# Two fused transformer blocks on one core: gate evacuation, key sums, roots and last stores moved in a written schedule

## The chip, the cores and the metric

The kernel runs as one program on one core of a Trainium2 chip. The metric is the device time of one execution in microseconds (us), taken from the chip and not from a host. Three executions of the kernel before are given, and one further execution that the hardware profiler recorded. The core has five engines that matter here: TensorE (PE, matrix products into eight PSUM banks), VectorE (DVE), ScalarE (ACT), GpSimd (POOL) and SyncE (SP, which only issues transfers). Each runs its own list of instructions in order, and they meet by semaphores.

## The reference, cut to what matters

The computation is two transformer-like blocks over 512 tokens of width 1024, in fp32, one behind the other. What the change touches lies in the hybrid mixer at the front of the first block, in the first norm of the second block, and in the last norm.

```python
def hybrid_mixer(h, w_in, ...):
    proj = h @ w_in
    gu, gv, q, k, v, gate, b_logit, a_logit = split_cols(proj, IN_SIZES)
    y_a = chunk_spatial_gating(gu, gv, gm_ln_g, gm_ln_b, gm_ws, gm_bs)
    qkv = silu(causal_dwconv(concatenate([q, k, v]), dn_conv))     # 4 taps
    q, k = l2norm(q), l2norm(k)                                    # per head
    g = -exp(dn_a_log) * softplus(a_logit + dn_dt_bias)
    o = gated_delta_rule(q, k, v, g, sigmoid(b_logit))             # 4 heads, 4 chunks of 128 tokens
    o = rmsnorm(o, dn_onorm) * silu(gate)
    return concatenate([y_a, o]) @ w_out
# gated_delta_rule, per head, chunk: decay = cumsum(g); m = strict(k_beta k^T * exp(decay_i - decay_j));
# solve (I + m) sol = [v_beta, k_beta exp(decay)]; then a recurrence over the chunks
def first_block(x, mem, ...):
    x = x + hybrid_mixer(rmsnorm(x), ...)
    x = x + memory_cross_attention(rmsnorm(x), rmsnorm(mem), ...)
    x = x + squared_relu_mlp(rmsnorm(x), ...)
    return rmsnorm(x, norm_final)
def second_block(x, ...):
    u = rmsnorm_2(x); proj = u @ w_in_2 + b_in_2    # conv branch, window attention (q, k, v with rope), merged
    x = x + merged @ w_mix_out;  x = x + (silu(conv(up)) * gate) @ w_ffn_down
    return rmsnorm_2(x)
```

## The kernel before, in words

**Products.** Every projection of 1024 (or fewer) input channels onto 128 output channels is a list of k-tiles (`KT` is 8), and each k-tile is three matrix products that together make an fp32 result: weight high part by activation high part, high by low, low by high (lines 1308 to 1310). One such product over 512 tokens takes about 0.23 us of PE, so half a projection, 12 products, takes 2.7 to 2.9 us. The high part of each weight tile is made by ACT (line 1604) and the low part by DVE (line 1884), four slots ahead; together these two are a "split".

**One list sets the order.** The function `schedule` writes one list of steps, and each engine's program walks that same list and emits its own part of each step. So a step that stands earlier in the list stands earlier on every engine that it uses. The steps around the change, with the lines of their instructions:

- `mm` is a piece of a projection. Its result lies in one of four projection banks, taken in turn, number j modulo 4. A bank is free again only when the step that evacuates it has run.
- `conv` evacuates a projection of q, k or v (DVE L1869), then ACT applies the first tap (L1667) and DVE the other three (L1876); `shape` is its silu on ACT (L1671).
- `gate` evacuates an output gate of the mixer (DVE L1869, into `gate`) and applies silu to it (ACT L1707).
- `sums` transposes a head's queries or keys on PE (L1381) and squares and sums them on ACT (L1679); DVE finishes them (L1974), and `norms` makes the scales (DVE L1980 to L1986).
- `decays` makes the cumulated decays of all heads (PE L1369, L1370; DVE L1954, L1957). `decay` of a head spreads them (PE L1235), and exponentiates (ACT L1713, with a table load; DVE L2030, L2034; ACT L1716).
- `strict` makes the strictly triangular matrix of a head (PE L1411, L1412; DVE L2042 to L2059), `turn` transposes the first inverse (PE L1420, DVE L2062), and `level_y` and `level_x` (PE L1437 and L1465, L1470; ACT L1721; DVE L2069, L2089, L2090) double the size of the inverted blocks, in six levels. At level 6 `level_y` has eight transposes with it (L1448, L1449), that DVE turns into `strict_t`, `decays_t` and `k_dec` (L2079 to L2082). `solve` closes a head. Two heads are on their way at a time, under the numbers 0 and 1 of their tiles.
- `statistics`, `normalise` and `mix` are the spatial gating of one group: transposes (PE L1388), mean and variance (DVE L2000 to L2004), normalising (DVE L2010), product. `mix_bias` is PE L1374 and DVE L1961.
- `square`, `root` and `row` are a norm: sums of squares tile by tile, then transposes and the root, then the row of scales spread over the partitions. In the first norm of the second block, `square` adds on POOL (L2344), with a second sum on POOL beside it (L2352), `root` is PE L1229 with small work on DVE and POOL (L2335, L2357), and `row` is PE L1235.

**Side banks.** The results of the small PE steps (`sums`, `decay`, `strict`, `turn`, levels, `statistics`, `mix`) share the other four PSUM banks, 4 to 7. They are given out in rotation, in the order of the list: a step takes the bank after the one before it, and PE waits until whoever read that bank last is done. So a step moved in the list changes which banks the steps behind it take, and for whom they wait.

**What sets the pace of the small steps.** `delta_head` is a generator that yields after each small step of a head; the main loop draws one piece of projection work (half a projection) from `filler`, then one step of each head in flight. The list `aside` holds small steps that are taken one at a time, one behind each half projection (`halves_and_aside`). So a step more in `aside` puts all behind it half a projection later.

**The end.** The last norm is applied to the second half of the tokens in parts, one DVE multiplication and one store for each part: `LAST_TILES` lists the k-tiles of a part (DVE L2319; the stores are issued by the queues of ACT, L1848, and SP, L2420).

## Time and profile before

| quantity | value |
|---|---|
| three executions | 1566.84, 1570.03, 1570.04 us; median 1570.03 us |
| the profiled execution | 1569.95 us |
| its span | 1568.2 us (1.75 us lie around it) |
| granted clock of TensorE, mean over the span | 0.993 |
| busy PE, DVE, ACT, POOL | 98%, 56%, 38%, 7% of the span |
| bytes moved | 146.70 MB, 94 GB/s on the mean |

The busy shares are means over the span. PE is busy nearly all of it, so the time can shrink only where PE stands still, where its clock is down, or at the two ends. A list of waits shows for whom an engine stood still and how long; the timeline shows each instruction with its start, its length, and, in brackets, the idle time right before it with the instruction that ended it. A row with "x4" groups four instructions. The granted clock is 1.00 at TensorE's full 2.4 GHz and 0.50 at 1.2 GHz.

### The profile page before, as it was taken

How to read it: one execution, taken by the hardware profiler on the slowest of the kernel's cores; microseconds unless marked ns; L12 is line 12 of the kernel's file. 1: busy time of each engine (PE TensorE's matmuls, PEld its weight loads, DVE VectorE, ACT ScalarE, POOL GpSimd, SP SyncE). 2: the span in 40 equal slices, each digit the busy share in tenths (PEclk: the TensorE clock that was granted, in tenths of full speed). 3: DMA queues.
4: the chain of work that ended last, by engine and by line, in shares of the span. 5: the costliest groups of instructions: out<-in, count | busy, mean ns of one | idle time of the engine just before them, and what ended most of it. 6: DMA issues, size and time to landing. Idle time of an engine off the chain costs nothing.

```text
span 1568.2 us, 20461 instructions
## 1 busy us (share of the span) xinstructions
PE 1543.0 (98%) x8150; PEld 1275.4 (81%) x8150; DVE 878.0 (56%) x1331; ACT 601.8 (38%) x975; POOL 104.9 (7%) x91
## 2 busy tenths in 40 slices
PE   9898999999999999999999999999999999999998
PEld 7687789888788888888888877877888888888887
DVE  7676666654364344445565777644555663564465
ACT  6534333533344132322446344432334331332233
POOL 0000111220030000000040010100002000000000
PEclk9998999999999999999999999999999999999999
DMA  7211113531132322232332223221332233222221
GB/s 265 68 55 41 55 55 109 188 107 59 36 113 90 107 90 99 94 104 78 108 108 81 81 81 108 74 94 62 107 113 89 95 107 102 87 99 102 95 71 64
DMA packets 44941, 146.70 MB, mean 94 GB/s; under 512 B 5040, under 2 KB 8368, under 8 KB 44720
## 3 DMA queue, kind: packets, MB, share of 16 engines
q1 hardware_dynamic: 42448, 141.80, 26.8%
q10 hardware_dynamic: 2400, 3.61, 0.7%
q8 instruction: 65, 1.06, 0.3%
q14 instruction: 28, 0.23, 0.1%
HBM read 143.29 MB, written 2.10 MB: 93 GB/s over the span
## 4 chain that ended last, share of the span: by engine, by line
PE 87%; DVE 6%; ACT 4%; issue 3%; DMA 1%; POOL 0%; SPq 0%; DVEq 0%; POOLq 0%; ACTq 0%
PE bank L1308 26%; PE bank L1310 26%; PE bank L1309 26%; DVE w_lo L1884 1%; PE bank L1526 1%; PE bank L1543 1%; ACT w_hi L1604 1%; DVE temp L1876 1%; PE bank L1437 1%; PE bank L1465 1%; DVE temp L1869 1%; PE bank L1470 1%; PE bank L1273 0%; PE bank L1275 0%; PE bank L1274 0%
## 5 line engine op out<-in xcount | busy, mean ns | idle before, releaser
L1308 PE MATMUL bank<-a_hi,w_hi 128*128 128x512 f32 (+1 forms) x1275 | 499.3, 392 | 6.0 <-DVE gate L1869 6.0
L1310 PE MATMUL bank<-a_hi,w_lo 128*128 128x512 f32 (+1 forms) x1275 | 491.3, 385 | 0.0
L1309 PE MATMUL bank<-a_lo,w_hi 128*128 128x512 f32 (+1 forms) x1275 | 491.2, 385 | 0.0
L1884 DVE TENSOR_TENSOR w_lo<-w_raw,w_hi 128x1024 fp32r<-128x1024 f32 (+2 forms) x259 | 330.3, 1276 | 171.4 <-ACT w_hi L1604 171.0
L1604 ACT ACTIVATE w_hi<-w_raw 128x1024 fp32r<-128x1024 f32 (+2 forms) x259 | 267.0, 1034 | 198.3 <-PE bank L1310 195.0
L1308 PEld LDWEIGHTS bank<-a_hi,w_hi 128*128 128x128 f32 x1275 | 240.6, 189 | 57.5 <-issue 9.9
L1310 PEld LDWEIGHTS bank<-a_hi,w_lo 128*128 128x128 f32 x1275 | 240.4, 189 | 48.5
L1309 PEld LDWEIGHTS bank<-a_lo,w_hi 128*128 128x128 f32 x1275 | 240.9, 189 | 45.6
L1308 PE MATMUL bank<-b_hi,w_hi 128*128 128x512 f32 (+1 forms) x720 | 276.7, 384 | 0.4 <-ACT b_hi L1744 0.4
L1309 PE MATMUL bank<-b_lo,w_hi 128*128 128x512 f32 (+1 forms) x720 | 275.1, 382 | 0.0
L1310 PE MATMUL bank<-b_hi,w_lo 128*128 128x512 f32 (+1 forms) x720 | 275.1, 382 | 0.0
L1308 PEld LDWEIGHTS bank<-b_hi,w_hi 128*128 128x128 f32 x720 | 135.3, 188 | 28.4 <-issue 1.7
L1310 PEld LDWEIGHTS bank<-b_hi,w_lo 128*128 128x128 f32 x720 | 135.3, 188 | 26.3
L1309 PEld LDWEIGHTS bank<-b_lo,w_hi 128*128 128x128 f32 x720 | 135.4, 188 | 26.1 <-issue 0.2
L2156 DVE TENSOR_TENSOR xs<-xs,bank 128x512 f32<-128x512 f32 (+1 forms) x88 | 55.9, 637 | 135.0 <-PE bank L1310 130.9
L1869 DVE TENSOR_TENSOR temp<-bank,rstd 128x512 f32<-128x512 f32 x101 | 69.4, 687 | 62.5 <-PE bank L1310 58.0
L1876 DVE SCALAR_TENSOR_TENSOR temp<-temp,columns 128x512 f32<-128x512 f32 x96 | 72.3, 753 | 35.0 <-ACT temp L1841 17.2
L2344 POOL TENSOR_TENSOR square_sum<-square_sum,square 128x512 f32<-128x512 f32 x28 | 39.5, 1410 | 612.5 <-ACT square L1639 612.5
L2134 DVE TENSOR_TENSOR b_lo<-temp,b_hi 128x512 fp32r<-128x512 f32 x62 | 42.9, 692 | 59.3 <-ACT b_hi L1744 59.0
L1744 ACT ACTIVATE b_hi<-temp 128x512 fp32r<-128x512 f32 x62 | 39.2, 633 | 82.5 <-DVE temp L2313 56.7
L1784 ACT ACTIVATE temp<-temp 128x512 f32<-128x512 f32 x32 | 20.2, 632 | 89.4 <-DVE temp L2209 89.4
L2335 POOL TENSOR_TENSOR narrow<-narrow,columns 128x4 f32<-128x4 f32 (+1 forms) x13 | 18.5, 1423 | 422.0 <-DVE narrow L1927 382.9
(317 smaller groups left out, 1196.2 us busy)
## 6 DMA issues: line engine op xcount, KB each, us to landing
w_raw<-weights_in SPq DMA_DIRECT2D x247, 512.0 KB, 3.2
w_raw<-weights_in SPq DMA_DIRECT2D x8, 384.0 KB, 2.9
x_first<-x_in SPq DMA_DIRECT2D x8, 256.0 KB, 5.8
xs<-x_in ACTq DMA_DIRECT2D x8, 256.0 KB, 5.0
w_raw<-weights_in SPq DMA_DIRECT2D x8, 256.0 KB, 2.7
mem_x<-mem_in SPq DMA_DIRECT2D x1, 1024.0 KB, 7.7
out<-xs SPq DMA_DIRECT2D x8, 128.0 KB, 1.8
w_raw<-front_in SPq DMA_DIRECT2D x5, 192.0 KB, 6.1
```

Of the source, the lines that this page charges most:

```text
L1308: pe.matmul(to, weights_hi[:, at], hi, start=k == k0, stop=False)
L1309: pe.matmul(to, weights_hi[:, at], lo, start=False, stop=False)
L1310: t = pe.matmul(to, weights_lo[:, at], hi, start=False, stop=k == k1 - 1)
L1604: act.activation(split_weights(n)[0][:, 0:size], raw[:, n % SLOTS, 0:size], ACT.Copy).then_inc(split_act.handle, 1)
L1744: act.activation(b_hi[:, b_slot(g, i), :], x, ACT.Copy).then_inc(b_act.handle, 1)
L1784: act.activation(temp("relu", n), temp("relu", n), ACT.Square).then_inc(relu_act.handle, 1)
L1869: return dve.tensor_tensor(to, full(name, n, k0)[0:to.shape[0], 0:width], scale[0:to.shape[0], 0:width], ALU.mult)
L1876: dve.scalar_tensor_tensor(acc, buf[:, at:at + S], weight(i), acc, ALU.mult, ALU.add).then_inc(done.handle, 1)
L1884: dve.tensor_tensor(lo[:, 0:size], raw[:, n % SLOTS, 0:size], hi[:, 0:size].bitcast(F32), ALU.subtract).then_inc(split_dve.handle, 1)
L2134: dve.tensor_tensor(lo, x, hi.bitcast(F32), ALU.subtract).then_inc(b_dve.handle, 1)
L2156: dve.tensor_tensor(xs[:, t, tokens], xs[:, t, tokens], full(name, t, k0)[:, 0:tokens.stop - tokens.start], ALU.add).then_inc(residual_dve ...
L2344: pool.tensor_tensor(total, total, square("square", n)[:, 0:total.shape[1]], ALU.add).then_inc(square_pool.handle, 1)
```

## The change

It has five parts. The first is at the front. The gates 0 and 1 are no longer taken from `aside` behind later half projections; their evacuation (`gate`) stands right behind `decays`, and their silu is a step of its own (`silu`) behind the silu of the third convolution of head 0. The projection that runs ahead is cut 2, 3, 3 k-tiles instead of 1, 5, 2. The queries' `sums 0` stands behind `strict 0` (it is `next(first)` a second time that puts it there), so that head 0, and with it every head behind it, is one step further ahead of the projections. Splits are taken at most one at a time.

The second is in the later heads: for heads 2 and 3 an empty entry is put into `aside` between the queries' and the keys' `sums`, so that the keys' stand half a projection later; the norms follow one entry on. The third is an empty entry ahead of the first `mix`. The fourth is at the first norm of the second block: the two `root` steps stand half a k2 projection and half a q2 projection earlier. The fifth cuts the last norm's parts from three (3, 3, 2 tiles) into four (1, 2, 3, 2 tiles).

```diff
@@ -59,7 +59,7 @@
 
 ON_DVE = (A_INPUT, *HALF_OF)
 
-LAST_TILES = [slice(0, 3), slice(3, 6), slice(6, KT)]
+LAST_TILES = [slice(0, 1), slice(1, 3), slice(3, 6), slice(6, KT)]
 
 
 
@@ -196,19 +196,20 @@
     def add(kind, n=0):
         out.append((kind, n))
 
-    def split_ahead(j):
-        while split[0] < min(j + LEAD + 1, N_LOADS) and (split[0] < SLOTS or split[0] - SLOTS in done or (
-                split[0] >= FIRST_EXTRA and PROJ["gate2", F2T - 1, 0] in done)):
-            add("split", split[0])
-            split[0] += 1
-
-    def project(name, n, k0=0, ka=None, kb=None):
+    def split_ahead(j, most=SLOTS):
+        for _ in range(most):
+            if split[0] < min(j + LEAD + 1, N_LOADS) and (split[0] < SLOTS or split[0] - SLOTS in done or (
+                    split[0] >= FIRST_EXTRA and PROJ["gate2", F2T - 1, 0] in done)):
+                add("split", split[0])
+                split[0] += 1
+
+    def project(name, n, k0=0, ka=None, kb=None, most=SLOTS):
         j = PROJ[name, n, k0]
         ka, kb = WEIGHTS[j][2] if ka is None else ka, WEIGHTS[j][3] if kb is None else kb
         if j < FRONT:
             done.add(j)
             return
-        split_ahead(j)
+        split_ahead(j, most)
         add("mm", (j, ka, kb))
         if kb == WEIGHTS[j][3]:
             done.add(j)
@@ -220,13 +221,13 @@
     aside, convolved, normed_heads = [], [], []
 
     def halves_and_aside(name, n):
-        project(name, n, kb=KT // 2)
+        project(name, n, kb=KT // 2, most=1)
         while convolved:
             add("shape", convolved.pop(0))
         if aside:
             aside.pop(0)()
         yield
-        project(name, n, ka=KT // 2)
+        project(name, n, ka=KT // 2, most=1)
         if aside:
             aside.pop(0)()
 
@@ -245,11 +246,15 @@
         for h in range(1, H):
             yield from conv_qkv(h)
             yield from conv_qkv(H + h)
-            aside.extend([lambda h=h: add("sums", h), lambda h=h: add("sums", H + h), lambda h=h: scaled(h)])
+            aside.append(lambda h=h: add("sums", h))
+            if h > 1:
+                aside.append(lambda: None)
+            aside.extend([lambda h=h: add("sums", H + h), lambda h=h: scaled(h)])
             yield from conv_qkv(2 * H + h)
             for n in GATES_BEHIND.get(h, ()):
                 yield from halves_and_aside("gate", n)
                 add("gate", n)
+                add("silu", n)
                 yield
         norm = memory_norm()
         for n in range(H):
@@ -261,7 +266,10 @@
                     add("spatial_u", n)
                 else:
                     add("spatial_v", n)
-                    aside.extend([lambda n=n: add("statistics", n), lambda n=n: add("normalise", n), lambda n=n: add("mix", n)])
+                    aside.extend([lambda n=n: add("statistics", n), lambda n=n: add("normalise", n)])
+                    if n == 0:
+                        aside.append(lambda: None)
+                    aside.append(lambda n=n: add("mix", n))
                 yield
                 if n or name == "gv":
                     next(norm, None)
@@ -273,6 +281,7 @@
         for _ in last:
             pass
         add("gate", H - 1)
+        add("silu", H - 1)
         yield
         while aside:
             aside.pop(0)()
@@ -374,19 +383,23 @@
     project("gate", 1, ka=KT // 2)
 
     ahead = PROJ["qkv", 1, 0]
-    add("mm", (ahead, 0, 1))
+    add("mm", (ahead, 0, 2))
     add("sums", H)
     add("decays")
-    add("mm", (ahead, 1, KT - 2))
+    for n in GATES_BEHIND[0]:
+        add("gate", n)
+    add("mm", (ahead, 2, 5))
     first = delta_head(0)
     next(first)
-    add("mm", (ahead, KT - 2, KT))
+    add("mm", (ahead, 5, KT))
     done.add(ahead)
+    scaled(0)
+    next(first)
     add("sums", 0)
-    scaled(0)
     add("shape", 2 * H)
+    for n in GATES_BEHIND[0]:
+        add("silu", n)
     filler = itertools.chain(projections(), first_memory_keys())
-    aside.extend([lambda: add("gate", 0), lambda: add("gate", 1)])
     in_flight, waiting = [first], list(range(1, H))
     while waiting or in_flight:
         next(filler, None)
@@ -471,11 +484,11 @@
             if k1 == FT:
                 normed(A_SECOND, n)
                 add("square2", n)
-    project("k2", 0)
+    project("k2", 0, kb=KT // 2)
     add("root", A_SECOND)
-    project("q2", 0, kb=KT // 2)
+    project("k2", 0, ka=KT // 2)
     add("root", A_TWICE)
-    project("q2", 0, ka=KT // 2)
+    project("q2", 0)
     add("row", A_SECOND)
 
     for n in (QT, 0):
@@ -1002,7 +1015,7 @@
-        gate_dve, gate_act = signal("gate_dve", "gate"), signal("gate_act", "gate")
+        gate_dve, gate_act = signal("gate_dve", "gate"), signal("gate_act", "silu")
@@ -1702,7 +1715,7 @@
-                elif kind == "gate":
+                elif kind == "silu":
                     q.wait_ge(*gate_dve.at(n))
                     act.activation(gate[:, n, :], gate[:, n, :], ACT.Silu).then_inc(gate_act.handle, 1)
```

The lines of the new kernel are 13 higher than those of the old from `project` on: L1869 is L1882, L1420 is L1433, and so on. Three places in the order of the instructions follow. In all of them `temp3`, `bank7` and the like are names with the number of the buffer.

**VectorE, from the decays of head 0 to its first turn.** Before, from the copy of the decays (L1954) on:

```order
L1954 COPY small<-bank5 128x32
L1957 TENSOR_TENSOR small<-small 128x16
L2030 TENSOR_TENSOR decays_t0<-bank6,small 128x512
L2034 TENSOR_TENSOR decays_t0<-decays_t0,matrices 128x512
...
L2047 TENSOR_TENSOR strict_b0<-bank4,decays_t0 64x256 x2
...
L1869 TENSOR_TENSOR temp3<-bank1,rstd 128x512
...
L1876 SCALAR_TENSOR_TENSOR temp4<-temp3,columns,temp4 128x512 x3
L1884 TENSOR_TENSOR w_lo<-w_raw,w_hi 128x1024 x2
L1869 TENSOR_TENSOR gate<-bank3,rstd 128x512
L1869 TENSOR_TENSOR gate<-bank0,rstd 128x512
L2062 COPY inv_b0<-bank6 128x256
```

Now, from the same copy on:

```order
L1967 COPY small<-bank5 128x32
L1970 TENSOR_TENSOR small<-small 128x16
L1882 TENSOR_TENSOR gate<-bank3,rstd 128x512
L1882 TENSOR_TENSOR gate<-bank0,rstd 128x512
L2043 TENSOR_TENSOR decays_t0<-bank6,small 128x512
...
L2060 TENSOR_TENSOR strict_b0<-bank7,decays_t0 64x256 x2
...
L1987 TENSOR_SCALAR narrow<-narrow 128x4
L1882 TENSOR_TENSOR temp3<-bank1,rstd 128x512
...
L1889 SCALAR_TENSOR_TENSOR temp4<-temp3,columns,temp4 128x512 x3
L1897 TENSOR_TENSOR w_lo<-w_raw,w_hi 128x1024
L2075 COPY inv_b0<-bank6 128x256
L1897 TENSOR_TENSOR w_lo<-w_raw,w_hi 128x1024
```

The two evacuations into `gate` have moved from behind two splits of weights, and behind the convolution, to a place ahead of the first multiplication of `decays_t0`. The copy into `inv_b0`, which is the turn of head 0, now has one split (`w_lo`) ahead of it rather than two and the gates.

**ScalarE, in the middle of heads 1 and 2.** `square0` or `square1` with `narrow` is the sum of squares of the keys or queries, `decays_t0` is head 2, `level_y1` is head 1. Before:

```order
L1671 ACTIVATE qkv<-temp4 128x512
L1679 ACTIVATE square1,narrow<-bank4 128x128 x4
L1721 ACTIVATE level_y1<-bank5 128x256
L1713 ACT_TABLE_LOAD
...
L1716 ACTIVATE decays_t0<-decays_t0 128x512
L1679 ACTIVATE square0,narrow<-bank7 128x128 x4
L1667 ACTIVATE temp2<-temp1,columns 128x512
L1604 ACTIVATE w_hi<-w_raw 128x1024
L1671 ACT_TABLE_LOAD
L1671 ACTIVATE qkv<-temp2 128x512
L1721 ACTIVATE level_y1<-bank4 64x256
```

Now:

```order
L1734 ACTIVATE level_y1<-bank5 128x256
L1726 ACT_TABLE_LOAD
...
L1729 ACTIVATE decays_t0<-decays_t0 128x512
L1680 ACTIVATE temp0<-temp4,columns 128x512
...
L1684 ACTIVATE qkv<-temp0 128x512
L1692 ACTIVATE square1,narrow<-bank5 128x128 x4
L1734 ACTIVATE level_y1<-bank6 128x256
L1680 ACTIVATE temp2<-temp1,columns 128x512
L1617 ACTIVATE w_hi<-w_raw 128x1024
L1684 ACTIVATE qkv<-temp2 128x512
L1692 ACTIVATE square0,narrow<-bank7 128x128 x4
L1734 ACTIVATE level_y1<-bank4 64x256
```

The exponential of head 2's decay (the first table load) stands one silu, one group of squares and one `level_y1` earlier, and the keys' squares from bank 7, once ahead of a scale, a split and a silu, stand behind all of them. On TensorE the first turn of head 2, which read bank 5 before, now takes bank 7. Before, on TensorE:

```order
L1448 MATMUL bank5<-matrices,qkv 128x128
L1449 MATMUL bank6<-matrices,qkv 128x128
L1308 MATMUL bank3<-a_hi,w_hi 128x512
...
L1374 MATMUL bank7<-ws,matrices 128x512 [waits strict_dve,ws_pool]
L1459 MATMUL bank4<-inv_t1,level_y1 64x64 [waits level_y_act]
L1459 MATMUL bank4<-inv_t1,level_y1 64x64 x3
L1420 MATMUL bank5<-matrices,inv_tb0 64x64 [waits level_y_dve]
L1420 MATMUL bank5<-matrices,inv_tb0 64x64 x7
L1308 MATMUL bank0<-a_hi,w_hi 128x512 [waits conv_dve,split_dve,split_act]
```

Now:

```order
L1462 MATMUL bank6<-matrices,qkv 128x128
L1461 MATMUL bank5<-matrices,qkv 128x128
L1462 MATMUL bank6<-matrices,qkv 128x128
L1433 MATMUL bank7<-matrices,inv_tb0 64x64 [waits sums_act]
L1433 MATMUL bank7<-matrices,inv_tb0 64x64 x7
L1321 MATMUL bank3<-a_hi,w_hi 128x512
...
L1387 MATMUL bank4<-ws,matrices 128x512 [waits level_y_act,ws_pool]
L1472 MATMUL bank5<-inv_t1,level_y1 64x64 [waits level_y_dve]
L1472 MATMUL bank5<-inv_t1,level_y1 64x64 x3
L1450 MATMUL bank6<-inv_b0,level_b01 64x64 [waits turn_dve]
```

The turn of head 2 stood behind the product of `ws` (`mix_bias`) and waited for DVE's `level_y_dve`; now it stands right behind the transposes and waits for `sums_act`, ACT's squares of that bank 7.

**TensorE, at the projections k2 and q2 and the roots.** Before, the last products of k2, the first root, half of q2, the second root:

```order
L1308 MATMUL bank0<-a_hi,w_hi 128x512 [waits stage_dve,stage_act]
...
L1308 MATMUL bank0<-a_hi,w_hi 128x512 [waits stage_dve,stage_act]
...
L1229 MATMUL bank4<-matrices,square_sum 128x128 [waits square_pool]
L1229 MATMUL bank4<-matrices,square_sum 128x128 x3
L1308 MATMUL bank1<-a_hi,w_hi 128x512 [waits residual_dve,split_dve,split_act]
...
L1229 MATMUL bank5<-matrices,square_sum2 128x128 [waits square2_pool]
L1229 MATMUL bank5<-matrices,square_sum2 128x128 x3
L1308 MATMUL bank1<-a_hi,w_hi 128x512
...
L1235 MATMUL bank6<-matrices,narrow 128x128 [waits root_dve,root_pool]
```
Now:

```order
L1321 MATMUL bank0<-a_hi,w_hi 128x512 [waits stage_dve,stage_act]
L1242 MATMUL bank7<-matrices,square_sum 128x128 [waits square_pool]
L1242 MATMUL bank7<-matrices,square_sum 128x128 x3
L1321 MATMUL bank0<-a_hi,w_hi 128x512 [waits stage_dve,stage_act]
...
L1321 MATMUL bank0<-a_hi,w_hi 128x512 [waits stage_dve,stage_act]
L1242 MATMUL bank4<-matrices,square_sum2 128x128 [waits square2_pool]
L1242 MATMUL bank4<-matrices,square_sum2 128x128 x3
L1321 MATMUL bank1<-a_hi,w_hi 128x512 [waits residual_dve,split_dve,split_act]
...
L1321 MATMUL bank1<-a_hi,w_hi 128x512
L1248 MATMUL bank5<-matrices,narrow 128x128 [waits root_dve,root_pool]
```
`bank7<-matrices,square_sum` (four transposes of the first root) stood behind all 24 products of k2 and now stands behind 12 of them, half a projection earlier; the second root likewise. The row (`narrow`, last of what is shown) stands behind the whole of q2 as before.

## Rows read from the trace of the kernel before

**Rows 1.** Waits of TensorE: engine, line, waited for, us in all, times, longest.

```profile
PE bank L1308 <- DVE gate L1869: 6.0, 1, 6.0
...
PE bank L1420 <- DVE k_dec L2082: 1.7, 1, 1.7
...
PE bank L1459 <- ACT level_y L1721: 0.5, 1, 0.5
```

**Rows 2.** Windows: busy us (instructions) PE, PEld, DVE, ACT, POOL; clock; DMA share; GB/s.

```profile
55.74:62.57 6.83, 2.89 (x7) 2.34 (x8) 5.96 (x10) 3.73 (x6) 0.00 (x0) 0.50 0.46 152
137.66:141.07 3.41, 3.41 (x17) 3.41 (x17) 1.64 (x5) 0.00 (x0) 0.93 (x1) 0.50 0.00 0
151.31:158.14 6.83, 6.21 (x28) 5.03 (x29) 4.41 (x10) 1.57 (x2) 0.00 (x0) 0.50 0.23 82
171.79:175.20 3.41, 2.04 (x37) 1.50 (x36) 3.19 (x8) 2.30 (x3) 0.00 (x0) 1.00 0.00 0
```

**Rows 3.** Timeline, TensorE, head 0: start, length, line, tiles, [idle before <- its ender].

```profile
39.02 0.63 PE L1381 MATMUL bank<-matrices,qkv 128*128 128x128 f32 x4 [0.63 <-ACT qkv L1671]
...
59.68 0.76 PE L1308 MATMUL bank<-a_hi,w_hi 128*128 128x512 f32 x1 [6.05 <-DVE gate L1869]
...
64.97 0.50 PE L1308 MATMUL bank<-a_hi,w_hi 128*128 128x512 f32 x1
...
67.86 0.60 PE L1381 MATMUL bank<-matrices,qkv 128*128 128x128 f32 x4
...
69.46 0.50 PE L1308 MATMUL bank<-a_hi,w_hi 128*128 128x512 f32 x1
```

**Rows 4.** Timeline, VectorE, strict 0 and the convolution behind it.

```profile
49.29 0.88 DVE L2047 TENSOR_TENSOR strict_b<-bank,decays_t 64x256 f32<-64x256 f32 x2
...
52.86 0.68 DVE L1869 TENSOR_TENSOR temp<-bank,rstd 128x512 f32<-128x512 f32 x1
...
56.58 2.35 DVE L1884 TENSOR_TENSOR w_lo<-w_raw,w_hi 128x1024 fp32r<-128x1024 f32 x2
```

**Rows 5.** Timeline, TensorE, heads 1 and 2.

```profile
124.61 0.68 PE L1465 MATMUL bank<-inv_tb,level_y 64*64 64x64 f32 x16
...
137.44 0.56 PE L1411 MATMUL bank<-qkv 128*128 128x128 f32 x2 [2.84 <-ACT square L1679]
...
145.20 0.48 PE L1308 MATMUL bank<-a_hi,w_hi 128*128 128x512 f32 x1
```

**Rows 6.** Timeline, ScalarE, head 2's decay and the squares of its keys.

```profile
132.27 1.28 ACT L1713 ACT_TABLE_LOAD   x1
133.56 0.60 ACT L1713 ACTIVATE temp<-bank 128x512 f32<-128x512 f32 x1
...
136.18 0.26 ACT L1679 ACTIVATE square<-bank 128x128 f32<-128x128 f32 x1
```

**Rows 7.** Timeline, TensorE, from the transposes of statistics 0.

```profile
167.63 0.60 PE L1388 MATMUL bank<-matrices,temp 128*128 128x128 f32 x4
...
174.18 0.68 PE L1470 MATMUL bank<-level_y,inv_tb 64*64 64x64 f32 x16 [1.37 <-DVE temp L2010]
```

**Rows 8.** Timeline, VectorE, normalise 0.

```profile
172.76 1.36 DVE L2010 TENSOR_SCALAR temp<-bank,ln_mean 128x128 f32<-128x128 f32 x4
```

**Rows 9.** Timeline, TensorE, k2, the roots and the row.

```profile
809.65 0.39 PE L1308 MATMUL bank<-a_hi,w_hi 128*128 128x512 f32 x1
...
815.09 0.60 PE L1229 MATMUL bank<-matrices,square_sum 128*128 128x128 f32 x4
...
822.60 1.09 PE L1235 MATMUL bank<-matrices,narrow 128*128 128x128 f32 x8 [0.96 <-POOL narrow L2357]
```

**Rows 10.** Timeline, GpSimd, its last square sum before the root.

```profile
813.45 1.40 POOL L2344 TENSOR_TENSOR square_sum<-square_sum,square 128x512 f32<-128x512 f32 x1 [3.04 <-ACT square L1639]
```

**Rows 11.** Timeline, VectorE, the last multiplications.

```profile
1562.33 2.42 DVE L2319 TENSOR_TENSOR xs<-xs,bank 128x768 f32<-128x768 f32 x3 [1.30 <-PE bank L1235]
```

**Rows 12.** Windows, the end: columns as in the second group.

```profile
1564.25:1567.45 3.20, 0.00 (x0) 0.00 (x0) 0.49 (x1) 0.00 (x0) 0.00 (x0) 0.53 0.97 328
```


## The prediction

> **What bounds the kernel now.** I read the busy shares first: TensorE is busy 98% of the span, so of the profiled 1569.95 us only its idle time, its slow clock and the two ends are to be had. Then the waits of TensorE in the part that the change moves: 6.0 us at a projection for DVE's evacuation of a gate, 1.7 us for `k_dec`, 0.5 us for ACT's `level_y` [rows 1]. Then the timeline around each, with the instruction that ended it. At 59.68 TensorE resumes after 6.05 us [rows 3]: this projection needs bank 3, which gate 0 (L1869) still holds. At 137.44 it resumes after 2.84 us for squares on ACT [rows 5], at 174.18 after 1.37 us for `normalise 0` [rows 7], at 822.60 after 0.96 us for a root on GpSimd [rows 9]. Last the granted clock, by windows: it is 0.50, that is 1.2 GHz, in 55.74 to 62.57, 137.66 to 141.07 and 151.31 to 158.14, each at or right behind a stall, and 1.00 in 171.79 to 175.20, which holds the 1.37 us stall [rows 2]. At half clock TensorE's busy time there is twice what it need be: losses of 2.89/2 = 1.4, 3.41/2 = 1.7 and 6.21/2 = 3.1 us. So a stall costs its length, and, if it is like the larger ones, 1.4 to 3.1 us behind it.
>
> Unit prices. Half a projection between small steps is 64.97 to 67.86 = 2.9 us; one group of four transposes with one `level_x` is 67.86 to 69.46 = 1.6 us [rows 3], which I divide 0.5 and 1.1 by their instructions. On DVE the strict matrix takes 49.29 to 52.86 = 3.6 us, a convolution, from its evacuation until its taps are done, 52.86 to 56.58 = 3.7 us [rows 4]. Four squares with their sums take 136.18 to 137.44 = 1.3 us on ACT [rows 5, 6].
>
> **Part 1, front, head 0.** Removed: the 6.05 us stall and 1.4 us of slow clock, and the 0.63 us that `sums 4` waits [rows 1 to 3]; 8.1 us in all. Added on DVE are two evacuations (the same instruction at 52.86 takes 0.68 us, and the next can start some 0.6 after it) before the first `decays_t` multiplication, where DVE waits for ACT's exponential anyway; they need the bank of gate 1, whose products have ended by then. I cost them at nothing; if that cover were gone they would be 1.2 to 1.4 us on the way to `strict 0`. What is late next is the turn of head 0: it is issued one piece of projection earlier on TensorE, but its copy on DVE stands behind conv 1 and one split. DVE starts on the strict matrix when TensorE has made it, which is 2.6 us earlier than 49.29, since the queries' four transposes and squares are no longer ahead. Then come 3.6 us of strict, 3.7 us of convolution and one split (half of the 2.35 us of the pair at 56.58, so 1.2 [rows 4]), and the copy, 0.4: 46.7 + 3.6 + 3.7 + 1.2 + 0.4 is 55.6, and with 0.25 us for the start of conv 1's taps behind ACT, which now also has the silus of both gates to do, 55.9. TensorE has by then done its projections and stands at `level_y (0, 1)` from 53.3. Stall 2.6 us, about as long as the 2.84 us one, so I add the slow clock of that size, 1.4 to 1.7: 4.1, with 0.3 for small waits at `decay 0` 4.4. Gain 8.1 - 4.4 = 3.7. Bounds: 6.5 if the clock holds and the stall is 1.2 shorter; 1 if both silus and the second split come ahead of the copy (1.2 + 1.2 us and more slow clock).
>
> **Part 2, later key sums, with head 2 one step ahead.** Removed: 2.84 + 1.7 at 137.44, then 0.5 + 1.7 + 3.1 around 151.93 [rows 1, 2, 5]: 9.8 us. Added: `decay 2` now stands ahead of conv 7 on DVE and of its silu on ACT, and the first turn of head 2 takes the bank of the keys' squares `sums 7`, which stand on ACT behind the silu of conv 11. From the start of the exponential's table load: DVE has its two multiplications done after about 3.3 (the exponentials end 0.6 before 136.18, 132.27 to 136.18 being 3.9 [rows 6]); conv 7 3.7; silu 0.6 and squares 1.3; one multiplication 0.7; strict 3.6; updates of the last level 1.2; conv 11 3.7; silu 0.6; squares 1.3. Sum 20.0 us. TensorE from the same moment: between `level_x (1, 4)` at 124.61 and the stall's start at 134.60 lie 10.0 us [rows 5]; less that `level_x` and one spread (1.1 + 0.4) 8.5, plus `strict 2`, half a projection and the last `level_y` with its transposes, which fill 137.44 to 145.20 less the slow clock's 1.7 = 6.1: 14.6, plus two short waits behind DVE and ACT, 0.9 together, 15.5 to 15.9. Stall 4.2 us, slow clock 1.7 as behind the 2.84 us stall, small waits 0.9: 6.9 us with rounding. The old stall at the `mix_bias` end goes, for the head is a step ahead. Gain 9.8 - 6.9 = 2.9. Bounds: 9.8 if ACT gets to the squares in time; -1 if the clock loss is the 3.1 us one and DVE lags one split (1.2) and an evacuation more.
>
> At this place the Trainium skill has a rule that speaks against the change, since more chains now wait behind an exponential. The row: the table load takes 1.28 us and the ACTIVATE starts right behind it, 132.27 + 1.28 = 133.55 against 133.56 [rows 6]. The page "ScalarE: Activation LUTs", section "What ACT_TABLE_LOAD costs", puts a switch at 1.283 us of load and 1.380 us of drain, 2.66 us. By that rule this stall would be 1.4 us longer and the sum of all parts 1.4 us worse; the trace has no such drain at the row, so the sum keeps 1.28.
>
> **Part 3, first mix later, heads 2 and 3.** `level_y (2, 3)` now takes the bank of `statistics 0`, free when `normalise 0` is done. Before, that was 167.63 to 172.76 + 1.36 = 174.12, 6.5 us after the statistics began [rows 7, 8]; the two updates of `level_x (2, 2)` now stand ahead, so I take 7.0. TensorE needs 0.5 (statistics) + 1.1 + 0.4 + 2.9 = 4.9. Stall 2.1 against 1.4 before; I price the slow clock at 0.7, half of the least seen, since none came behind 1.37 us and one came behind 2.84. Two more short waits behind `k_turn` and `normalise` of the next head, where each bank moves on by one, I take at 0.9 together. New loss 1.4 + 1.1 over before with the clock: 2.4. Bounds: 0 to -5 (another stall of 2.8 with its clock).
>
> **Part 4, roots half a projection earlier.** GpSimd's last square sum ends at 813.45 + 1.40 = 814.85 [rows 10]. The first half of k2 is done at 809.65 + (815.09 - 809.65)/2 = 812.4 [rows 9]. Before, the root came at 815.09 and found its sum ready by 0.2 us; now TensorE waits 2.5 us. Then remain half of k2, q2 whole and two roots: 3 halves of 2.8 with 0.7 for the roots, row at 824.1. Before it came at 822.60, behind a wait of 0.96, so the root's chain is no longer what it waits for. Loss 824.1 - 822.6 = 1.5, and 1.3 of slow clock for a stall just under 2.84: -2.8. Bounds: -1.5 (no clock), -4.6 (3.1).
>
> **Part 5, last stores.** The three multiplications take 2.42 us from 1562.33 [rows 11], and the stores' data run from 1564.25 to 1567.45 at a share of 0.97 [rows 12]: the transfer is the bound, and its start follows the first part. With one tile first instead of three, 2/8 of 2.42 = 0.6 us less before the first issue. A fourth issue costs some 0.1 to 0.6, and unless one queue serves two short stores better than one, I keep +0.2, from -0.3 to +0.6. The same skill's page "DMA: Bandwidth & Descriptors", section "Anatomy of one DMA", gives about 2.0 us fixed for each DMA (on GpSimd's path). By it a further store that lay alone would cost 2.0; the packets at 0.97 show that fixed times overlap here. I keep +0.2.
>
> **Sum.** 3.7 + 2.9 - 2.4 - 2.8 + 0.2 = +1.6 us. 1569.95 - 1.6 = 1568.35; the median before is 0.08 above the profiled execution: 1568.4. A measurement of this kernel can tell about 0.2%, 3.1 us, from no change; the forecast lies within.
>
> **Rivals.**
> (a) The new waits are covered. The turn of head 2 finds its bank free, since ACT runs its scale and split earlier than I chain them, and `level_y (2, 3)` too. Then parts 2 and 3 are +9.8 - 1 (small waits) and 0, and the sum 3.7 + 8.8 - 2.8 + 0.2 = 9.9: 1560.1; with only half of that stall gone (2.1, and its 1.7 of clock) 1564.6. For it: DVE is busy 56% and ACT 38%, and each price above was put end to end. Against: the squares stand behind the silu, which stands behind the taps, in the order itself.
> (b) Slower. Stalls that start the slow clock: at the first root TensorE stands still 2.5 us in the midst of dense products, and if each of the new stalls (front 2.6, turn 4.2, level 2.1, root 2.5) draws the 3.1 us loss seen behind 151.93 in place of the 1.4, 1.7, 0.7 and 1.3 that I gave them, the loss grows by 7.3: 1575.7. From two of the four on, by about 3.3, it is 1571.7, slower than before. For it: the loss came behind a stall of 1.66 with 0.54 before it. Against: it was 1.4 and 1.7 behind longer ones.
> (c) It does nothing: the 6 us at the front only move to the turn's copy, because the splits behind it (`most=1`) hold DVE or the copy waits for conv 1 in full. Then part 1 is 0 to +1, the sum -1 to -2: 1571.5.
>
> **How the numbers follow.** Forecast 0.40: faster in 0.08 of it, within 0.2% in 0.27, slower in 0.05. (a) 0.32, nearly all faster. (b) 0.14, slower in 0.12. (c) 0.14: within 0.10, slower 0.04. Together faster 0.40, same 0.39, slower 0.21. The range reaches over (a)'s half case towards its end and over (b) from two stalls: 1561.0 to 1572.5; the forecast's own is 1565 to 1571.
>
> **What would show it.** In the new trace: no wait of a projection for a gate, and one of 2 to 3 us at the first `level_y` for the turn's copy; the wait for `sums` at the turn of head 2, about 4 us (its absence is (a)); a wait of some 2 us at `level_y (2, 3)` for `normalise`; 2.5 us at the first root for GpSimd's square sum, and none at the row; windows at 0.50 behind each. It would be wrong if the new waits are under 1 us each or if a stall over 3 us appears at a place that I don't name, in the later gating groups above all, where every bank has moved on.

## The result, and the profile after

The changed kernel takes 1572.4 us (median of 12 executions, 1569.5 to 1573.1), the kernel before 1569.1 us (12 executions, 1566.8 to 1570.6). The ratio is 1.0018, with a 95% interval of 1.0009 to 1.0026: the change makes the kernel slower by some 2.8 us (3.3 us by the medians). I had forecast 1568.4 us, 1.6 us faster than the profiled execution before, with a range of 1561.0 to 1572.5 us: the direction came out wrong, and the time at the range's slow end.

The profiled execution of the changed kernel took 1569.49 us, with a span of 1567.8 us; that of before took 1569.95 us. Read side by side, the two profiles say "0.5 us faster". How that goes with a slower median is the first lesson of this case. The waits of TensorE after the change (engine and line, waited for, us in all, times, the longest; lines are 13 higher than before):

```profile
PE bank L1433 <- ACT square L1692: 4.5, 1, 4.5
PE bank L1450 <- DVE temp L2023: 3.6, 2, 2.1
PE bank L1450 <- DVE inv_b L2075: 2.5, 1, 2.5
PE bank L1242 <- POOL square_sum L2357: 2.3, 1, 2.3
...
PE bank L1242 <- DVE k_dec L2095: 1.0, 1, 1.0
PE bank L1493 <- DVE temp L2023: 0.8, 1, 0.8
```

The 6.0 us wait for a gate, the 1.7 us one for `k_dec` and the 0.5 us one for `level_y` at its old place [rows 1] are gone, and so is the 2.8 us one for squares [rows 5]. In their place stand 4.5 us at the turn of head 2, 3.6 us in two waits for `normalise`, 2.5 us for the turn's copy of head 0 and 2.3 us for GpSimd's square sum. The timeline of TensorE at these places, with the wait in brackets:

```profile
55.49 0.68 PE L1450 MATMUL bank<-inv_b,level_b 64*64 64x64 f32 x16 [2.49 <-DVE inv_b L2075]
```

```profile
141.25 1.12 PE L1433 MATMUL bank<-matrices,inv_tb 64*64 64x64 f32 x16 [4.50 <-ACT square L1692]
```

```profile
168.20 0.68 PE L1450 MATMUL bank<-inv_b,level_b 64*64 64x64 f32 x16 [2.08 <-DVE temp L2023]
...
189.03 0.68 PE L1450 MATMUL bank<-inv_b,level_b 64*64 64x64 f32 x16 [1.50 <-DVE temp L2023]
...
202.71 0.41 PE L1242 MATMUL bank<-matrices,temp 128*128 128x128 f32 x2 [0.99 <-DVE k_dec L2095]
...
210.99 0.46 PE L1493 MATMUL bank<-inv_t,strict_t 128*128 128x128 f32 x2 [0.81 <-DVE temp L2023]
```

```profile
811.59 0.88 PE L1242 MATMUL bank<-matrices,square_sum 128*128 128x128 f32 x4 [2.35 <-POOL square_sum L2357]
```

The granted clock of the same execution, by windows (columns as in [rows 2]: busy us of PE, PEld, DVE, ACT, POOL, then the clock):

```profile
55.00:61.00 6.00, 5.51 (x66) 4.65 (x67) 4.91 (x10) 2.65 (x5) 0.00 (x0) 1.00 0.53 178
139.45:146.25 6.80, 5.00 (x25) 4.07 (x26) 3.91 (x11) 3.33 (x11) 1.01 (x1) 0.50 0.22 77
168.00:175.00 7.00, 6.80 (x78) 5.88 (x79) 5.59 (x13) 3.20 (x6) 1.27 (x2) 1.00 0.01 2
811.87:815.28 3.41, 3.41 (x12) 2.73 (x11) 2.76 (x3) 0.00 (x0) 1.44 (x2) 0.50 0.17 24
```

Half clock came at two of these four places (a last stretch, from 1562.8 us to the span's end, meets no work of TensorE; every profile has one at its end), for a loss of 5.00/2 + 3.41/2 = 4.2 us, against 6.2 us in the profiled execution before. Behind the 2.5 us wait at the front and the 2.1 us wait of the gating the clock stayed at 1.00. So the time without slow clock is 1569.95 - 6.2 = 1563.7 us before and 1569.49 - 4.2 = 1565.3 us after: on that scale the change costs 1.6 us. Beside the drawn clock, one execution can tell a difference to about 1 us, as the start of the kernel varies too (see the second profile below).

### The profile page after: what moved, and what is told of

The parts are those of the page before. It is cut to its first block, busy times and chain, and to the rows that moved or that the text cites. A ratio compares the mean times of both kernels' runs of the same rounds, so it can differ in the third digit from the quotient of the medians.

```text
span 1567.8 us, 20470 instructions
## 1 busy us (share of the span) xinstructions
PE 1542.2 (98%) x8150; PEld 1274.0 (81%) x8150; DVE 877.5 (56%) x1332; ACT 601.6 (38%) x975; POOL 104.8 (7%) x91
## 4 chain that ended last, share of the span: by engine, by line
PE 89%; issue 4%; DVE 4%; ACT 2%; POOL 1%; POOLq 0%; DVEq 0%; ACTq 0%
PE bank L1321 26%; PE bank L1322 26%; PE bank L1323 26%; PE bank L1539 1%; PE bank L1556 1%; DVE temp L1889 1%; POOL square_sum L2357 1%; PE bank L1478 1%; PE bank L1450 1%; PE bank L1286 0%; PE bank L1288 0%; PE bank L1287 0%; PE bank L1483 0%; DVE temp L1882 0%; PE bank L1596 0%
## 5 line engine op out<-in xcount | busy, mean ns | idle before, releaser
L2169 DVE TENSOR_TENSOR xs<-xs,bank 128x512 f32<-128x512 f32 (+1 forms) x88 | 55.9, 636 | 134.9 <-PE bank L1323 130.8
L1882 DVE TENSOR_TENSOR temp<-bank,rstd 128x512 f32<-128x512 f32 x101 | 69.3, 686 | 56.4 <-PE bank L1323 51.8
```

Of the source, the lines that this page charges most:

```text
L1882: return dve.tensor_tensor(to, full(name, n, k0)[0:to.shape[0], 0:width], scale[0:to.shape[0], 0:width], ALU.mult)
L2169: dve.tensor_tensor(xs[:, t, tokens], xs[:, t, tokens], full(name, t, k0)[:, 0:tokens.stop - tokens.start], ALU.add).then_inc(residual_dve ...
```

## The experiments

Twelve runs follow, of eleven edited kernels and of the changed one once more, with 5 to 11 executions each. They ran in three groups (the first on one chip, the other two on another), each with the kernel before beside it: the changed kernel, the roots, the key sums and the extra step; then the first mix, the front alone and two of the better versions; then the rest. The runs of before had medians of 1569.0, 1569.25 and 1569.0 us, so I compare across the groups, though the changed kernel ran only in the first. "Ratio" is to before, "below the changed kernel" is a difference of medians to its run here.

**The clock: the changed kernel again.** No edit.

> The changed kernel, unchanged, for a second profile and as the reference of its neighbours. The profile of the first was of an execution of 1569.5 us, and 8 of 12 executions took 1571.6 to 1573.1. Theory A (most executions have one more stretch at half clock, behind the 2.5 us wait at the front or the 2 us wait of the gating): median 1572.4, and a profiled execution above 1572 shows a third stretch at 0.50, worth about 2.9 us. Rival B (the difference is spread over the program, as transfers or slow starts): such a profile shows two stretches as the first did, and lags the first profile little by little.

Measured: 1571.8 us, ratio 1.0020 (1.0010 to 1.0030). Its profiled execution took 1571.6 us, 2.1 us more than the first, and has the same waits to within 0.1 us: 4.5, 3.6 in two, 2.5 and 2.4 us. Its windows:

```profile
56.13:59.54 3.41, 3.18 (x21) 2.71 (x22) 2.40 (x6) 1.50 (x4) 0.00 (x0) 0.50 0.69 205
141.45:148.27 6.82, 4.73 (x25) 3.85 (x26) 4.20 (x11) 3.32 (x11) 1.01 (x1) 0.50 0.21 77
813.87:817.28 3.41, 3.41 (x11) 2.82 (x12) 2.93 (x3) 0.00 (x0) 1.44 (x2) 0.50 0.07 18
```

A third stretch stands at the front. It is worth 3.18/2 = 1.6 us, not the 2.9 us that I expected; together 5.7 us, so 1565.9 us without slow clock, 0.6 us above the first profile. That rest lies at the start: the first transposes of head 0 begin at 39.40 us here and at 38.84 us in the first profile. Over the 13 profiles of the changed kernel and its variants, whose order is the same up to there, they begin between 38.8 and 40.0 us. This is Theory A, though the profiled execution was not one above 1572: the stalls are the same in each execution, and which of them draws half clock is not.

**The roots.** In the diffs of the experiments, + is what the experiment has and - what the changed kernel has.

```diff
-    project("k2", 0, kb=KT // 2)
+    project("k2", 0)
     add("root", A_SECOND)
-    project("k2", 0, ka=KT // 2)
+    project("q2", 0, kb=KT // 2)
     add("root", A_TWICE)
-    project("q2", 0)
+    project("q2", 0, ka=KT // 2)
```

> The changed kernel with only the k2/q2 roots put back where they stood. Theory A (the root now waits for GpSimd's square sum and pulls the slow clock behind it): the 2.3 us wait and the window at clock 0.50 behind it vanish, the row is at the old distance from k2's first product, and the time is 3.0 us below the changed kernel (1572.4), so about 1569.4, ratio to before 1.000. Rival B (that loss is given back later, since the row waited for GpSimd anyway): within 0.7 us of the changed kernel, 1572.

Measured: 1569.0 us, ratio 1.0004 (0.9995 to 1.0012), 2.7 us below the changed kernel beside it. The 2.3 us wait is gone, and the row waits 1.0 us for GpSimd again. Theory A holds: 3.0 expected, 2.7 found. Half of it is wait. The rest I put down to the clock: of the seven profiles that have the root's wait, four have a stretch of 3.4 us behind it, worth 1.7 us each, so 1.0 us on the mean. This one profile can't show it by itself, since it has three stretches of 3.4 us at other places: at the front, at the turn of head 2 and behind `statistics 0`.

**The key sums.**

```diff
             aside.append(lambda h=h: add("sums", h))
-            if h > 1:
-                aside.append(lambda: None)
             aside.extend([lambda h=h: add("sums", H + h), lambda h=h: scaled(h)])
```

> The changed kernel without the empty entry between a head's query and key sums. Theory A (turn 2 waits 4.5 us because the keys' squares of head 3 stand behind the silu of conv 11): the squares come half a projection earlier, ahead of that silu, the wait and the slow clock behind it (2.6 us) are gone, less 1 to 2 us for a next wait: 5 to 6 us below the changed kernel, about 1567. Rival B (DVE is late there whatever the squares do, as it has strict 2 and conv 11 in a row, and the wait only changes its name): the stall of 3 to 4.5 us stands at the first product of ws or at the turn with another releaser, and the time is within 1.5 us of the changed kernel.

Measured: 1568.6 us, ratio 0.9996 (0.9987 to 1.0005), 3.2 us below the changed kernel. The 4.5 us wait is gone, but two take its place, of 0.96 us at `level_x (1, 5)` for `strict 2` on DVE and of 1.12 us for `k_dec`:

```profile
134.79 0.68 PE L1481 MATMUL bank<-level_y,inv_tb 64*64 64x64 f32 x16 [0.96 <-DVE strict_t L2058]
...
145.60 0.50 PE L1470 MATMUL bank<-inv_t,level_y 64*64 64x64 f32 x5 [1.12 <-DVE k_dec L2093]
```

Between the two theories: the squares were the cause of the long wait, and DVE stands some 1 us behind them.

**The same squares, otherwise.** The step for the keys of head 3 and the silu of conv 11 swap places.

```diff
-        while convolved:
-            add("shape", convolved.pop(0))
-        if aside:
-            aside.pop(0)()
+        if convolved == [2 * H + 3]:
+            aside.pop(0)()
+            add("shape", convolved.pop(0))
+        else:
+            ...
```

> The changed kernel with the key sums of head 3 ahead of the silu of conv 11 in the list, two neighbours swapped. Theory A (turn 2 waits 4.5 us because ACT squares those keys only behind that silu, which itself needs DVE's taps): ACT squares them right behind the split, some 1.9 us earlier, the wait falls to about 2.6 us, and the slow clock behind it from 6.8 us to 3.4 us in length: 2.5 to 3 us below the changed kernel, 1569. Rival B (another buffer or the sum on DVE holds the bank): the wait stays at 4.5 us and so does the time.

Measured: 1569.5 us, ratio 1.0003 (0.9994 to 1.0012), 2.3 us below the changed kernel. On ACT the squares now start right behind the split and end ahead of the silu:

```profile
138.01 1.04 ACT L1621 ACTIVATE w_hi<-w_raw 128x1024 fp32r<-128x1024 f32 x1
138.96 0.26 ACT L1696 ACTIVATE square<-bank 128x128 f32<-128x128 f32 x1
...
140.50 0.63 ACT L1688 ACTIVATE qkv<-temp 128x512 f32<-128x512 f32 x1 [0.42 <-DVE temp L1893]
```

The wait fell from 4.50 to 2.41 us, where 2.6 was expected. In the changed kernel the same squares started at 140.07, behind the silu at 139.54:

```profile
137.05 1.04 ACT L1617 ACTIVATE w_hi<-w_raw 128x1024 fp32r<-128x1024 f32 x1
139.54 0.63 ACT L1684 ACTIVATE qkv<-temp 128x512 f32<-128x512 f32 x1 [1.45 <-DVE temp L1889]
140.07 0.26 ACT L1692 ACTIVATE square<-bank 128x128 f32<-128x128 f32 x1
```

**Head 0's extra step.**

```diff
-    scaled(0)
-    next(first)
     add("sums", 0)
+    scaled(0)
```

> The changed kernel with only the head's extra step taken back (sums 0 ahead of strict 0, norms behind it). Theory A (being a step ahead makes the small steps arrive before DVE and ACT are done): the 2.5 us wait for the turn's copy and the 4.5 us wait at turn 2 shrink to under 1 us each and their slow clock goes with them; some 6 us below the changed kernel, about 1566. Rival B (the step ahead is what took the 6 us and the 2.8 us stalls of the kernel before away): one of those comes back, and the time is not below 1571.

Measured: 1566.9 us, ratio 0.9990 (0.9981 to 0.9999): 4.9 us below the changed kernel and faster than before. The turn's copy is waited for 1.9 us, not 2.5, so it did not shrink to under 1 us. The time is near the 1566 of Theory A, but not for its reason, that both waits shrink to under 1 us; Rival B is refuted, as neither old stall came back. The 4.5 us wait is gone; the same squares now hold up the product of `ws`, for 2.2 us:

```profile
PE bank L1241 <- POOL square_sum L2356: 2.4, 1, 2.4
PE bank L1386 <- ACT square L1691: 2.2, 1, 2.2
PE bank L1482 <- DVE temp L2022: 2.0, 2, 1.4
PE bank L1449 <- DVE inv_b L2074: 1.9, 1, 1.9
PE bank L1449 <- ACT square L1691: 1.6, 1, 1.6
```

**The first mix.**

```diff
                     aside.extend([lambda n=n: add("statistics", n), lambda n=n: add("normalise", n)])
-                    if n == 0:
-                        aside.append(lambda: None)
                     aside.append(lambda n=n: add("mix", n))
```

> The changed kernel with only the first mix back, half a projection earlier. Theory A (the waits for normalise 0 and 1, 2.1 and 1.5 us, come from the bank of the statistics being the one that the next level takes, and that comes with the extra step, not with the later mix): the waits stay, and the time is within 1 us of the changed kernel (1572). Rival B (the later mix is what moved the banks): both waits fall to under 1 us, and the time is 3 us lower.

Measured: 1569.5 us, ratio 1.0003 (0.9994 to 1.0012), 2.2 us below the changed kernel. Neither theory in full: the 2.08 us wait for `normalise 0` stays, the 1.50 us one for `normalise 1` is gone. The first comes with the extra step (with the step back and the mix later, in the run above, `normalise` is waited for 1.4 us at most, as before), the second with the later mix.

```profile
PE bank L1448 <- DVE temp L2021: 2.1, 1, 2.1
```

**Another bank for the levels behind the statistics.**

```diff
+SKIP = {(4, 'level_y', (2, 3)): 1, (4, 'level_y', (2, 5)): 1}
 class Turns:
...
         for kind, n in SCHEDULE:
+            at += SKIP.get((size, kind, n), 0)
```

> The changed kernel, where level_y (2, 3) and level_y (2, 5) each take one bank further in the rotation, so that they don't take the bank of statistics 0 and 1; nothing else in the order of the steps moves. Theory A (the 2.1 and 1.5 us waits are for the bank alone, not for data): both are gone, 3.6 us and the slow clock that they draw in part of the executions, so 4 to 5 us below the changed kernel (1571.8): 1567.3. Rival B (DVE is late there in any case, so the next step that needs DVE waits as long): a wait of 1.5 us or more at level_x (2, 3), and less than 1.5 us of gain.

Measured: 1567.1 us, ratio 0.9995 (0.9986 to 1.0004), 4.7 us below the run of the changed kernel by the medians and 3.9 us by the ratios (1.0020 - 0.9995). The order of the steps is that of the changed kernel, and both waits for `normalise` ahead of a `level_y` are gone; 4.5, 2.5 and 2.4 us stay as they were:

```profile
PE bank L1437 <- ACT square L1696: 4.5, 1, 4.5
PE bank L1454 <- DVE inv_b L2079: 2.5, 1, 2.5
PE bank L1246 <- POOL square_sum L2361: 2.4, 1, 2.4
```

So these 3.6 us of wait, and the clock that they draw, were for the bank and for no data: Theory A.

**The front alone, and better versions.** Step, key sums, mix and roots all back; what is left of the change is the gates' evacuation, the splits and the last stores:

> The kernel before with only the first gates' evacuation moved ahead of decay 0, their silu apart, splits one at a time and the four last stores (head step, key sums, mix and roots all back). Theory A (the parts are nearly additive): the front's 6 us and its slow clock go, a wait of 1 to 2 us for the turn's copy stays, the 2.8 us and 1.7 us waits of heads 1 and 2 return: 4 to 5 us below before (1569.0), about 1564.5. Rival B (what is gained at the front is given back at the next waits, since DVE and ACT set the pace of the heads, not TensorE): within 1.5 us of before.

Measured: 1564.3 us, ratio 0.9970 (0.9958 to 0.9982), 5.0 us faster than before. The waits of 2.84, 1.66 and 1.37 us are there again, and 1.92 us for the turn's copy is all that is left of the 6.05. Theory A to within 0.3 us by the median, with six executions between 1562.2 and 1567.3 us.

```profile
PE bank L1419 <- ACT square L1687: 2.8, 1, 2.8
PE bank L1445 <- DVE inv_b L2070: 1.9, 1, 1.9
PE bank L1428 <- DVE k_dec L2090: 1.7, 1, 1.7
PE bank L1478 <- DVE temp L2018: 1.4, 1, 1.4
```

Only step and roots back:

> The changed kernel with the head's extra step and the roots back (the run without the step took 1566.9, the one without the root's move was 2.7 us below the changed kernel). Theory A (the root's stall costs 2.3 us and its clock wherever the heads stand, so the two are additive): 1564.2. Rival B (the slow clock behind the root is only passed on to another stall, so that without it others draw it more often): 1565.5 to 1567.

Measured: 1563.1 us, ratio 0.9960 (0.9947 to 0.9974). 1.1 us better than the sum of parts; the one profile has no slow stretch but the one at the end, in the last 7 us. Against the run with the roots back alone (1569.0) it prices the extra step at 5.9 us; 4.9 us was its price with the roots moved. It is the dearest piece of the change.

Only key sums and roots back:

> The changed kernel with the key sums and the roots back; the head's extra step stays. Theory A (additive): 1568.6 - 2.7 = 1565.9. Rival B as in the run beside it: 1567 or more. If the extra step is worth its place, this one is below the run with the step back; I expect it above, by 1 to 2 us, as the waits for normalise (2.1 and 1.5 us) stay.

Measured: 1565.8 us, ratio 0.9972 (0.9961 to 0.9983), where 1565.9 was expected. It lies 2.7 us above the run with step and roots back, where I expected 1 to 2, and 1.5 us above front and stores alone, from which it differs by the extra step and the later mix together. So the extra step is not worth its place here either; its price without the later key sums was not measured apart from the mix.

Step and roots back, and later key sums for head 3 alone:

```diff
-            if h > 1:
+            if h > 2:
                 aside.append(lambda: None)
```

> The run with step and roots back (1563.1), and the key sums half a projection later for head 3 alone, not for head 2. Theory A: the 1.64 us wait of level_y (1, 3) for the squares of head 2's keys goes and nothing takes its place, since the kernel before had none there: 1561.3. Rival B (the stall moves to another place, as DVE sets the pace): 1563 again.

Measured: 1562.5 us, ratio 0.9963 (0.9951 to 0.9976). The 1.64 us wait is gone, with nothing in its place, but of the 1.8 us expected the median shows 0.6, within the spread.

The same, with those key sums ahead of the silu of conv 11:

> As the run beside it (step and roots back, later key sums for head 3 alone), and those key sums ahead of the silu of conv 11. Theory A: also the 2.24 us wait of mix_bias for these squares falls to under 0.5 us: 1559.5, 0.6% below before. Rival B (as the idle time is cut, what is left is the two blocks' floor and the slow clock is drawn by whatever stall is left): no better than 1561.5.

Measured: 1561.8 us, ratio 0.9955 (0.9942 to 0.9967): the fastest, 7 us below before and 10 us below the changed kernel, though its interval overlaps those of the three beside it. 1559.5 was expected. The 2.24 us wait for squares became a wait of 1.16 us for `level_y` just behind; it was not cut to 0.5:

```profile
PE bank L1486 <- DVE temp L2026: 2.0, 2, 1.4
PE bank L1453 <- DVE inv_b L2078: 1.9, 1, 1.9
...
PE bank L1475 <- ACT level_y L1737: 1.2, 1, 1.2
```

## Why the prediction was wrong

Two terms of the sum failed, both in parts 2 and 3: slow clock of one execution was booked as a gain that comes each time, and the further short waits of the moved steps were put at 1.8 us in all and came to 4.4. The parts, each as it was priced and as it came out, follow. Prices of single parts are differences of medians.

- **Part 1, front: the mechanism right.** Gain 3.7 forecast. The kernel with front and stores alone, without the extra step, gained 5.0, with the stall for the copy at 1.9 us; with the head a step ahead, as forecast, it was 2.49 (2.6 forecast; the copy was forecast to end at 55.9 and ended at 54.93 + 0.42 = 55.35). The gates' evacuation on DVE was hidden as argued, from 41.77 on, and DVE's next step began at 43.12, when ACT's exponential had ended at 43.09:

```profile
41.77 1.27 DVE L1882 TENSOR_TENSOR gate<-bank,rstd 128x512 f32<-128x512 f32 x2
43.12 0.69 DVE L2043 TENSOR_TENSOR decays_t<-bank,small 128x512 f32<-128x512 f32 x1
...
54.93 0.42 DVE L2075 COPY inv_b<-bank 128x256 f32<-128x256 f32 x1
```

- **Part 2: the place right, the sign wrong.** The wait at the turn of head 2 was forecast at 4.2 us and is 4.50, for the squares on ACT, as said. What failed is the step "Removed: 2.84 + 1.7 at 137.44, then 0.5 + 1.7 + 3.1 around 151.93: 9.8 us". The 5.0 us of waits did go. The other 4.8 us were slow clock as it fell in one execution, booked as a certain gain: in the profile of front and stores alone the same waits drew 3.4 us (3.42/2 and 3.36/2). The new stall was charged 1.7 and drew 2.5 and 2.4, and 1.5 to 2.8, or 2.1 on the mean, over the five profiles that have it. And the extra step, which this part's title has, got no price of its own; it took 4.9 to 5.9 us. The later key sums took 3.2 us with the step, and without it, together with the later mix, nothing that the medians show (1563.1 against 1564.3).
- **Part 3: the mechanism right, cut off too early.** I worked out one bank, that of `statistics 0` (2.1 us forecast, 2.08 found), and charged "0.9 together" to what follows. That wait stayed when the mix was put back, so it belongs to the extra step and not to this part. The rotation repeats the pattern at each group: `statistics 1` cost 1.50, and then 0.99 and 0.81 us came at the first norm's transposes and at a `solve`. The sentence "in the later gating groups above all, where every bank has moved on" named the danger, and nothing in the sum paid for it. The part's own sum is off as well: "1.4 + 1.1" is 2.5, not 2.4, and the 0.9 named just before would make it 2.3.
- **Part 4: right.** 2.8 us forecast, 2.7 measured; wait 2.5 forecast, 2.35 found.
- **Part 5: consistent, not tested by itself.** From the first of the last multiplications to the span's end it took 1568.2 - 1562.33 = 5.9 us before and 1567.8 - 1562.07 = 5.7 us after, 0.2 us less as forecast. Counted from TensorE's last product it is 5.7 us in each of the 13 profiles with four parts and 5.9 in the one profile of before. The stores' data ran at a DMA share of 0.83 where it was 0.97 [rows 12], so what starts sooner does not fully end sooner:

```profile
1562.07 2.48 DVE L2332 TENSOR_TENSOR xs<-xs,bank 128x256 f32<-128x256 f32 x4 [1.30 <-PE bank L1248]
```

```profile
1563.50:1567.10 3.60, 0.00 (x0) 0.00 (x0) 1.04 (x2) 0.00 (x0) 0.00 (x0) 0.50 0.83 282
```

Parts 2 and 3 together, with the extra step, were +0.5 us in my sum. The changed kernel with the roots back (1569.0) against front and stores alone (1564.3) makes them -4.7 us. In the two profiles, TensorE stands still 4.7 us more between 30 and 300 us, 13.8 against 9.1, and the slow clock is about the same, 4.9 and 5.1 us. These 5.2 us are the error, less the 1.1 us by which front and stores came out better; by the medians the whole error is 1.6 + 3.3 = 4.9 us, and the two runs of the changed kernel lie 0.6 us apart.

It splits in two. Without slow clock my sum had +0.7 us for the change (3.8 at the front, -0.2 for part 2, -1.6, -1.5, +0.2), and the profiles say -1.6 and -2.2: 2.6 us on the mean. Some 2 us of it are idle time: between 30 and 300 us TensorE stood still 13.9 us before and 13.8 after, where my sum had 2.0 less. The waits that I had not listed (1.50, and 0.99 + 0.81 + 0.65 + 0.40 in place of the 1.8 charged in parts 2 and 3) are 2.5 us; two waits of before that I had not listed either, 0.36 and 0.46, went. The remaining 0.6 us I can't place, but for the later start of the second profile. The second half is slow clock: I had forecast 1.0 us less of it, and by the medians there is 1.4 us more, 1569.1 - 1563.7 = 5.4 us before and 1572.4 - 1565.6 = 6.8 us after. This second half rests on two profiles of the changed kernel and one of before.

Of the rivals, (b), more slow clock at the new stalls, is nearest: slower, through the same four places. But it is only half of the loss, and at none of them did I see the 3.1 us that it named; the most was 2.8. (a) and (c) did not happen.

As to table loads, the trace after agrees with that before: at head 2's exponential, on the chain to the turn's stall, the load takes 1.28 us and the next work starts right behind it, 121.12 + 1.28 = 122.40 against 122.42.

```profile
121.12 1.28 ACT L1726 ACT_TABLE_LOAD   x1 [2.78 <-PE bank L1248]
122.42 0.60 ACT L1726 ACTIVATE temp<-bank 128x512 f32<-128x512 f32 x1
```

The rule of the Trainium skill ("ScalarE: Activation LUTs", "What ACT_TABLE_LOAD costs") of 1.4 us more for a drain would have made the turn's forecast stall of 4.2 us 5.6; it was 4.5.

## What to carry to other kernels

A buffer rotation is a hidden order: whoever inserts or moves one step must list, for every later step until the pattern closes, whose buffer it now takes and when that is free. One bank skipped at two steps was worth some 4 to 4.7 us here, with no work moved. Compare two profiles with the slow clock taken out (busy time at half clock, halved), and price the clock by medians of several executions, since a single profile books a draw as if it were a property. A bundle of edits is worth taking apart even when its net is near zero: here the front without its extra step, with the stores, brought 5 us, and the rest took 8: 2.7 the roots, and some 5 the extra step with what was moved beside it. The parts don't add up one by one: the later key sums cost 3.2 us with the extra step and nothing that could be seen without it.

## What the runs showed of the hardware

The same stall draws half clock in one execution and not in the next. The 2.5 us wait at the front, in the eight profiles that have it, was followed by a stretch at 0.50 in six; the 2.1 us wait for `normalise 0` in four of seven; the 2.35 us wait at the root in four of seven; the 4.5 us wait in all five. Draws at neighbouring stalls seem not to be independent: the wait for `normalise 0` drew none in the three profiles with a 6.8 us stretch at the turn of head 2, some 27 us earlier, and one in each of the four without; seven profiles are few, and why is open. In the better versions the 1.9 us wait at the front drew one in two profiles of five and the 2.2 us wait for squares in one of three. The single waits of 1.37, 1.50 and 1.64 us drew none in any profile, but one of 1.16 us, with one of 0.38 us right behind, did; the one of 1.66 us, with a wait of 0.5 or 0.3 us just ahead of it (0.7 us of work between), drew one in both profiles that have it. The stretches were 3.4 or 6.8 us long, and the long ones stood behind the 4.5 us wait, the 6.05 us one and the one of 1.66 us of the first profile. Splitting idle time into shorter waits may be worth as much as cutting it: step and roots back has some 10 us of listed waits, front and stores alone some 8, and the first is no slower; its one profile lost nothing to half clock ahead of the last 7 us, that of the other 5.1 us. That this is the clock's doing was not tested by itself.
